# A decoder trunk with 16 experts: splitting the second half of the down weights on GpSimd, for three float32r products

## The reference, cut to what matters

```python
for e in range(N_EXPERTS):                               # 16
    h = jax.nn.silu(xt @ e_wg[e]) * (xt @ e_wu[e])       # (576, 1024) @ (1024, 512), twice
    y = y + combine[:, e:e + 1] * (h @ e_wd[e])          # (576, 512) @ (512, 1024)
...
x = layer_norm(DN_ALPHA * x + moe(x, ...), ln_g[2], ln_b[2])
```

## Time and profile before

| | us |
|---|---|
| median of 3 runs | 1592.98 (1591.44 to 1595.31) |
| the profiled execution | 1593.02 |
| its span, first to last instruction | 1591.2 |
| busy in the span: TensorE | 1436.9 (90%) |
| VectorE | 782.9 (49%) |
| ScalarE | 514.3 (32%) |
| GpSimd | 298.1 (19%) |
| mean granted TensorE clock | 0.957 |

### The profile page before, as it was taken

One profiled execution on the slowest core, in us unless ns is written; L12 is line 12 of the kernel. 1 busy time (PEld: TensorE's weight loads), 2 busy tenths in 40 slices (PEclk: granted clock), 3 DMA queues, 4 the chain that ended last, 5 costly groups with the idle time before them and its releaser, 6 DMA issues.

```text
span 1591.2 us, 20322 instructions
## 1 busy us (share of the span) xinstructions
PE 1436.9 (90%) x8037; PEld 1199.5 (75%) x8037; DVE 782.9 (49%) x1162; ACT 514.3 (32%) x772; POOL 298.1 (19%) x234
## 2 busy tenths in 40 slices
PE   5998889899789788999999989999897799999985
PEld 4887888888778676989998867765685677777762
DVE  6204437362545467632221430244336688887786
ACT  1123341513431343311110011333123566666640
POOL 5111132313314131323332000001000100000030
PEclk9999999998899898999999989999998899999997
DMA  9302232422122121242225311235254699999941
GB/s 328 99 27 74 79 96 77 118 84 78 53 82 71 49 80 40 62 130 80 80 59 195 124 54 53 80 116 207 62 222 153 240 381 394 390 390 396 391 152 61
DMA packets 182172, 234.89 MB, mean 148 GB/s; under 512 B 6224, under 2 KB 125705, under 8 KB 181953
## 3 DMA queue, kind: packets, MB, share of 16 engines
q1 hardware_dynamic: 154848, 170.90, 31.7%
q0 software_dynamic: 12384, 43.56, 8.0%
q10 hardware_dynamic: 14849, 19.16, 3.5%
HBM read 213.98 MB, written 19.36 MB: 147 GB/s over the span
## 4 chain that ended last, share of the span: by engine, by line
PE 48%; DVE 3%; DMA 2%; ACT 2%; issue 1%; POOL 0%; POOLq 0%; DVEq 0%; SPq 0%; ACTq 0%
PE bank L1114 46%; ACT kv_t L744 1%; PE bank L1606 1%; DMA ring<-in_w_out_dram 1%; DMA early_rows<-expert_rows,ints 0%; DVE x_tok L2490 0%; DVE small L1739 0%; DVE x_tok L2496 0%; POOL early_rows L2673 0%; DMA xg<-x_scratch,table 0%; PE bank L1598 0%; PE bank L1138 0%; PE bank L1422 0%; DVE x_tok L2398 0%; DVE x_tok L1751 0%
## 5 line engine op out<-in xcount | busy, mean ns | idle before, releaser
L1114 PE MATMUL bank<-x_hi,z_weights_hi 128*128 128x288 f32 x960 | 307.1, 320 | 9.1 <-DVE ob L1903 5.5
L1114 PE MATMUL bank<-x_lo,z_weights_hi 128*128 128x288 f32 x960 | 290.5, 303 | 0.0
L1114 PE MATMUL bank<-x_hi,z_weights_lo 128*128 128x288 f32 x960 | 290.1, 302 | 0.0
L2232 DVE TENSOR_TENSOR expert_weights_lo<-mring,expert_weights_hi 128x2048 fp32r<-128x2048 f32 x80 | 181.8, 2287 | 54.2 <-ACT expert_weights_hi L1007 54.0
L1114 PEld LDWEIGHTS bank<-x_hi,z_weights_hi 128*128 128x128 f32 x960 | 189.0, 197 | 15.6 <-issue 6.3
L1114 PEld LDWEIGHTS bank<-x_lo,z_weights_hi 128*128 128x128 f32 x960 | 188.6, 196 | 2.6
L1114 PEld LDWEIGHTS bank<-x_hi,z_weights_lo 128*128 128x128 f32 x960 | 187.7, 195 | 0.0
L1007 ACT ACTIVATE expert_weights_hi<-mring 128x2048 fp32r<-128x2048 f32 x80 | 153.4, 1918 | 78.7 <-PE bank L1114 78.7
L2544 POOL CAST z_weights_hi<-z_weights 128x1024 fp32r<-128x1024 f32 x60 | 65.7, 1094 | 592.3 <-PE bank L1114 365.8
L2546 POOL TENSOR_TENSOR z_weights_lo<-z_weights,z_weights_hi 128x1024 fp32r<-128x1024 f32 x60 | 147.4, 2456 | 6.4 <-POOL z_weights_hi L2544 2.9
L1114 PE MATMUL bank<-ob,branch_weights 128*128 128x288 f32 (+1 forms) x512 | 134.5, 405 | 0.0
(11 more groups left out here) (419 smaller groups left out, 2303.7 us busy)
## 6 DMA issues: line engine op xcount, KB each, us to landing
mring<-in_e_wg_dram SPq DMA_DIRECT2D x32, 1024.0 KB, 8.5
mring<-in_e_wu_dram SPq DMA_DIRECT2D x32, 1024.0 KB, 9.4
mring<-in_e_wd_dram SPq DMA_DIRECT2D x32, 1024.0 KB, 8.0
z_weights<-in_w_in_dram SPq DMA_DIRECT2D x60, 512.0 KB, 3.9
branch_weights<-in_w_branch_dram SPq DMA_DIRECT2D x32, 256.0 KB, 3.2
kv_k<-in_cache_mem_k_dram POOLq DMA_DIRECT2D x8, 1024.0 KB, 7.6
kv_v<-in_cache_mem_v_dram POOLq DMA_DIRECT2D x8, 1024.0 KB, 5.5
expert_rows<-y_out ACTq DMA_DIRECT2D x14, 512.0 KB, 6.9
```

The lines of the kernel that those rows point to most:

```text
L1114: return pe.matmul(out, lhsT, rhs, start=start, stop=stop)
L2232: dve.tensor_tensor(m_lo[slot][:], mring[:, slot, :], m_hi[n % NHI][:].bitcast(F32), ALU.subtract).then_inc(m_lo_done, 1)
```

## The change

For experts 0 to 12 (`WHOLE = 13`) the second half of the down weights is split too. GpSimd does it (`split_rest`): a cast writes hi into one of two new buffers, a subtraction writes lo over the chunk in the ring. The two buffers lie on `x_tok`, whose rows are in DRAM by then. TensorE makes 12 float32r products (`down_rest`) in place of the 4 float32 ones. The hidden values' second half needs hi and lo as well: ScalarE's second copy in `hidden_out` writes float32r, and VectorE makes one more subtraction, 128 x 256, from PSUM (`h2_lo`). Since `x_tok` is overwritten, ScalarE's queue reads it back from `x2_d` in pass 14, and ScalarE scales it by alpha in pass 15, behind `last_hi(0)`; VectorE's five scalings in passes 12 to 15 go, and each `early_add` waits for its scaled tile. Experts 13 to 15 keep the plain product.

```diff
+        h2_hi = place("hidden_rest_hi", 34816, [P, 2, 2, P], F32R)
+        h2_lo = place("hidden_rest_lo", 47040, [P, 2, 2, P], F32R)
+        d2_hi = [place(f"down_rest_hi{k}", 42944 + SLOT * k, [P, SLOT], F32R) for k in range(2)]
...
+                if e == WHOLE + 1:
+                    act.wait_ge(full[6], moe_base[6] + WHOLE)
+                    for t in range(NT):
+                        act.dma_start(x_tok[0:TILES[t], t, :], x2_d[P * t:P * t + TILES[t], :]).then_inc(x_back, 16)
+                if e == NE - 1:
+                    act.wait_ge(x_back, 16 * NT)
+                    for t in range(NT):
+                        act.activation(x_tok[0:TILES[t], t, :], x_tok[0:TILES[t], t, :], ACT.Copy, scale=ALPHA).then_inc(x_scaled, 1)
...
+            def down_rest(u, hi, lo):
+                hi, lo = slot_rows(hi[:], True), slot_rows(lo[:], True)
+                for s in range(2):
+                    cols = slice(512 * s, 512 * s + 512)
+                    for k in range(2):
+                        m = split_product(bank[5 + s][:, :], (h2_hi[:, u, k, :], h2_lo[:, u, k, :]), (hi[:, k, cols], lo[:, k, cols]),
+                                          False, k == 1)
+                    m.then_inc(full[5 + s], 1)
...
-                    pe.wait_ge(*chunk_landed(("d", e - 1, 1)))
-                    down_second(1 - u, mring[:, chunk_slot[("d", e - 1, 1)], :])
+                    if e - 1 < WHOLE:
+                        pe.wait_ge(d2_lo_done, e)
+                        down_rest(1 - u, d2_hi[(e - 1) % 2], m_lo[chunk_slot[("d", e - 1, 1)]])
+                    else:
...
-            later.update({11 + t: (lambda t=t: scaled(t)) for t in range(1, NT)})
...
                 wait(dve, h_hi_done, n + 1)
+                if isinstance(n, int) and n < WHOLE:
+                    dve.tensor_tensor(h2_lo[:, u], bank[4][:, 256:512].rearrange("p (a b) -> p a b", a=2),
+                                      h2_hi[:, u].bitcast(F32), ALU.subtract)
...
                 dve.wait_ge(yab_landed[t], 32)
+                dve.wait_ge(x_scaled, t + 1)
...
+            def split_rest(e):
+
+                pool.wait_ge(*chunk_landed(("d", e, 1)))
+                if e >= 2:
+                    pool.wait_ge(full[6], moe_base[6] + e - 1)
+                raw, lo = mring[:, chunk_slot[("d", e, 1)], :], m_lo[chunk_slot[("d", e, 1)]]
+                pool.tensor_copy(d2_hi[e % 2][:], raw).then_inc(d2_hi_done, 1)
+                pool.wait_ge(d2_hi_done, e + 1)
+                pool.tensor_tensor(lo[:], raw, d2_hi[e % 2][:].bitcast(F32), ALU.subtract).then_inc(d2_lo_done, 1)
+
             for e in range(NE):
                 if e >= 2:
                     pool.wait_ge(full[3], moe_base[3] + e - 1)
                 gather(table[:, e:e + 1], e % 2).then_inc(xg_landed[e % 2], 16)
+                if 2 <= e < WHOLE + 2:
+                    split_rest(e - 2)
```

More of the change, by code:

```diff
@@ L326 @@
 OVER_AT = 5
+WHOLE = 13
 LAST_AT = {7: (0, 0), 8: (0, 1), 9: (1, 0), 10: (1, 1)}
@@ L551, in trunk @@
         ld_masks = sem("masks_landed")
+        d2_hi_done, d2_lo_done = sem("down_rest_hi"), sem("down_rest_lo")
+        x_back, x_scaled = sem("residual_landed"), sem("residual_scaled")
         x_in = [sem(f"x{t}_landed") for t in range(NT)]
@@ L1018, in gate_out, with hidden_out @@
                 act.activation(hs[:, u, :], bank[0][:, :], ACT.Silu).then_inc(free[0], 1)
-            def hidden_out(wait, n, u):
+            def hidden_out(wait, n, u, rest=hT):
                 wait(act, full[4], n + (moe_base[4] + 1))
                 act.activation(hT_hi[:, u], bank[4][:, 0:256].rearrange("p (a b) -> p a b", a=2), ACT.Copy)
-                act.activation(hT[:, u], bank[4][:, 256:512].rearrange("p (a b) -> p a b", a=2), ACT.Copy).then_inc(h_hi_done, 1)
+                act.activation(rest[:, u], bank[4][:, 256:512].rearrange("p (a b) -> p a b", a=2), ACT.Copy).then_inc(h_hi_done, 1)
             def down_out(wait, n, out):
@@ L1061, in _ @@
                 if e:
-                    hidden_out(plain_wait, e - 1, (e - 1) % 2)
+                    hidden_out(plain_wait, e - 1, (e - 1) % 2, h2_hi if e - 1 < WHOLE else hT)
                 split_hi(ahead + 1)
@@ L1657, in _ @@
                         hidden_turned(plain_wait, e, u)
-                    pe.wait_ge(*chunk_landed(("d", e - 1, 1)))
-                    down_second(1 - u, mring[:, chunk_slot[("d", e - 1, 1)], :])
+                    if e - 1 < WHOLE:
+                        pe.wait_ge(d2_lo_done, e)
+                        down_rest(1 - u, d2_hi[(e - 1) % 2], m_lo[chunk_slot[("d", e - 1, 1)]])
+                    else:
+                        pe.wait_ge(*chunk_landed(("d", e - 1, 1)))
+                        down_second(1 - u, mring[:, chunk_slot[("d", e - 1, 1)], :])
             down_ready(plain_wait, NE - 1)
@@ L2348, in keep_one_hots @@
                     dve.tensor_tensor(w[:, 0:1], w[:, 0:1], w[:, 1:2], ALU.add).then_inc(hot_kept, 2)
[L2350 to L2354, removed]
             def overflow_table():
```

## The result

The changed kernel takes 1635.89 us (median of 4 runs, 1634.13 to 1639.59) against 1594.14 (1591.44 to 1596.75) before: ratio 1.0265, 95% interval 1.0239 to 1.0291, 2.65% slower. The profiled execution took 1634.13 us, its span is 1632.3 us, 41.1 more than before.

What follows compares the result with a forecast made beforehand. TensorE was taken to bound the expert stage, VectorE having 3.5 us spare a pass. Longer passes 34, chores 6, pass 13 -0.7 and end of stage 4 gave +43 on 1593.0: 1636 us, own range 1622 to 1646.

Steps and rivals of the forecast that it cites:

- (1): TensorE's second-half down products: twelve float32r in 2.75 us against 3.41 for four full-precision, saving 0.66 us a pass.
- (2): GpSimd's cast and subtraction at 2048 wide: 2.07 + 4.79 = 6.86 us for an expert, 89.2 us for 13.
- (3): VectorE instructions with two SBUF inputs and GpSimd's exclude each other, whole instructions in turn; operands in PSUM are exempt.
- the walk: Pass 11 followed instruction by instruction with loads landing after 8.0 us: 21.3 us instead of 18.46.
- (4): Passes lengthened by GpSimd's turns on VectorE's path: +2.85 us each, 12 passes, +34 us, product saving included.
- (5): VectorE's routing chores, formerly hidden by TensorE, count when behind GpSimd's turn: 0 to 18.9 us, taken as 6.
- (6): End of the stage: additions wait for ScalarE's late scaling, +4.0 us; store about 2.5 us late, hidden.
- The signs: Profile after: weight splits up to 4.5 to 7 us, PSUM readers unchanged, TensorE idle 3 us a pass, VectorE busy 90%.
- A: Rival: GpSimd's turns fall into VectorE's gaps, TensorE stays the bound, 1588.4 us; chance 0.06.
- B: Rival: chores and more PSUM readers lie beside GpSimd, or loads land favourably, +1.3 us a pass, 1613 us; chance 0.21.
- C: Rival: GpSimd's instructions a third longer than twice the half width, chores counting in full, 1652 us; chance 0.15.
- D: Rival: three products as long as the full-precision one, GpSimd's work all hidden, about 1593 us; chance 0.02.

Runs made afterwards that it cites:

- kernel 1: Changed kernel without GpSimd's cast and subtraction, the twelve products reading buffers of zeros: 1594.52 us, ratio 0.9996 to the kernel before.
- Kernel 4: Changed kernel with the cast moved to ScalarE at each pass's end, GpSimd only subtracting a pass later: 1614.51 us, ratio 1.0131 to before.
- kernel 2: Changed kernel with WHOLE = 0, so no chunk split by GpSimd, late read-back and ScalarE's scaling kept: 1599.19 us, ratio 1.0035 to before.

## Why the prediction was right, step by step

The forecast was 1636, the result is 1635.9. The mechanism was right. That the total fits to 0.1 us is luck: the waiting was forecast some 17 us too high, and the 17 us of products that take longer were not in it.

- **What bounds**: right. VectorE's spare 3.5 us a pass was the right thing to watch. TensorE never waited for a DMA (share 0.89 in the stretch). But the landing of the chunk sets when GpSimd starts, and so which of VectorE's instructions it meets.
- **(1) Products**: 0.66 us a pass forecast, 0.73 measured (18.46 to 17.73 in kernel 1).
- **(2) GpSimd's durations**: 2.07 and 4.79 forecast from half the width, 1.89 and 4.59 measured when nothing holds them up. Twice the half was 4 to 9% too much.
- **(3) The lock**: right, and the walk has the right order: cast, split, GpSimd's subtraction, split. PSUM readers were exempt, as read from the earlier trace rows. It works both ways: 10.5 us for GpSimd's pair in pass 12 holds 4 us of waiting for VectorE.
- **(4) 2.85 us for each of 12 passes**: the sum with (5) held, its composition did not. The two passes without chores, 11 and 12, lasted 24.4 and 19.6 us, 22.0 in the mean, where I had 21.3. I took the products at full clock and all of the loss as waiting. With the 17.7 us pass of kernel 1 the forecast 21.3 means 3.6 us of idle each. Measured are 32.2 us of idle in all, 2.7 for each of the 12, and 17 us in which the same products took longer, most of it by the lower clock, a term missing in my sum. Passes at full clock are shorter than forecast or the same (19.6 to 21.5), pass 11 with its two falls is longer (24.4). The load of pass 12 was there at 5.0 us into the pass and not at 8.0, so the fixed pattern that I continued did not come; long and short passes follow one another. The walk also starts pass 11 at 1446.45 where the trace before has 1445.93: the whole walk is 0.5 us late, its lengths are not touched.
- **(5) Chores, 6 of 0 to 18.9 us**: no run separates them from (4). That they can wait a whole turn was right: a 128x160 operation took 4.73 us. Kernel 4 doesn't either: passes 11 and 12, without chores, take 18.4 and 17.9 us there, pass 4 with some 23.3, but pass 7 with some 18.1 and pass 6 with next to none 22.1. What they cost stays open.
- **Sum of (4) and (5)**: 40 forecast, 40.1 measured. The 40 us over the kernel before are 47 over kernel 1's passes, and I took all of them as waiting. Measured are 47 as well, but 30 of waiting and 17 of products that take longer. The missing clock and the overcounted waiting cancelled.
- **(6) End of the stage**: the first addition starts behind the scaling and not on the gathered rows, as forecast, and the last low part ends 3.97 us later (forecast 4.0). But these 3.97 us aren't what the end waits for: the path runs through the down product of expert 15, which starts 4.2 us later and, not foreseen, takes 1.1 us longer at 0.69 of the clock. The store lands 3.5 us late where I took 2.5, and is hidden as forecast. In sum +5.4 us against 4; kernel 2 measured the tail alone at +0.35%, 5.6 us.
- **Pass 13**: -0.7 forecast, -0.6 in it and -0.4 in pass 14.
- **Start of the stage**: 3.3 us earlier in the profiled execution, with the same work before it. The other kernels scatter from 1243.2 to 1246.6 (kernel 1 apart). I take it for chance, which no run shows; without it the parts add to +44.4.
- **The signs**: splits up to 6.70 us, readers of PSUM at 0.68, TensorE waiting for VectorE's gathered rows and splits came as announced. VectorE was busy 88% of the stretch, not 90.
- **Rivals**: A (1588.4) needed GpSimd's turns in VectorE's gaps; the row of kernel 4's pass without chores shows that this happens with one turn of 4.6 us, not with two. B (1613) wanted more of VectorE's work beside GpSimd's turns, C (1652) longer instructions of GpSimd: the stretch and the durations say no to both. D is excluded by kernel 1, where the passes are 6.8 us shorter than before.

## What to carry to other kernels

Spare time on an engine is not free for its neighbour: price the neighbour's instructions as whole turns taken out of the busy engine's order, small instructions included, and look for where both meet earlier in the same kernel. The same split given to ScalarE and VectorE, 2.3 us of added work on the engine next to the bound, gained 2.7 us over 13 passes where GpSimd's lost 40. To waits put into TensorE's stream add the lower clock that may follow, here 17 us of longer products beside 30 of waiting, most of it the clock; and before moving a transfer ahead of another in a queue, ask who waits for the second.

## What the runs showed of the hardware that I had not expected

- Behind waits of 1.82 to 4.33 us of TensorE the granted clock was 0.50 to 0.58 in the next 4 us six times in 13 passes (from 1271.03, 1299.88, 1345.13, 1425.38, 1475.59 and 1492.85 us), mostly at 1.2 GHz. It stayed at 1.00 behind six other waits of 1.49 to 2.76 us. Two waits of 2.76 us, those that end at 1449.92 and at 1492.85, stand on either side: a fall behind a wait of that length is not sure, and what decides is open. (The stage itself begins at the low clock, in both kernels: 0.50 in the 4 us ahead of 1240.52.)
- VectorE's shortest operations wait as long as its longest: 128x1 elements took 4.18 us, 128x160 4.73 us, beside a GpSimd subtraction of 4.6.
- GpSimd at 128x2048 took 1.89 us for a cast and 4.59 for a subtraction of two SBUF tensors, where VectorE took 2.29 and ScalarE's cast 1.91.
- A 512 KB store behind 2.36 MB of read-back in one queue landed in 6.1 us instead of 2.6.
